# A state-space mixer on one core: decay exponents formed by accumulating DMA transfers instead of matmuls, their exponentials moved to other places in ScalarE's order, all convolved tiles gated through Tanh

## The chip, the cores and the metric

One NeuronCore of one Trainium2 chip. The kernel is one launch. The metric is the device time of that launch in microseconds (us), as the median over runs; a profiled execution has its own time and its own span (first to last instruction).

## What is computed

Two transformer-like blocks run one after the other on 256 tokens of width 1024, all in float32: six feed-forward parts on the main stream, one on a context stream, an attention and recurrence mixer, a gated convolution mixer and a state-space mixer (SSD) with a Fourier branch. The change lies in the state-space mixer alone. Its core, per direction, cut to what matters:

```
xbc = silu(centred_conv3(xbc, conv_w) + conv_b)          # split in cm, xs, bm
dt  = softplus(dt_raw + dt_bias);  a = -exp(a_log)
a_cs = cumsum(dt * a)                                    # per head, inside chunks of 128 tokens
seg = exp(where(lower, a_cs[l] - a_cs[s], -inf))         # 128 x 128 per head, chunk, direction
cb  = einsum('lgn,sgn->gls', cm, bm)                     # 4 groups of 3 heads
y_diag = einsum('gls,grls,sgrp->lgrp', cb, seg, xs * dt)
y_off  = cm . h_prev . exp(a_cs)                         # what comes in from the other chunk and the context
y = y_f + flip(y_b) + d_skip * xs;  y = group_rms_norm(y * silu(z)) * w;  out = y @ w_out
```

12 heads of 64 columns in 4 groups, state size 128, 2 chunks of 128 tokens, 2 directions.

## The kernel before

All weights lie in one stream of 529 slots of 128 x 1024 float32 values (512 KB). SyncE loads a slot into one of 4 `raw` buffers. ScalarE rounds it to float32r (`w_hi<-raw`, L1145), VectorE takes the rest (`w_lo<-raw,w_hi`, L1784), into rings of 8 slots, and TensorE multiplies three times for each product (hi by hi, lo by hi, hi by lo). Each engine has one queue in program order; the order of every engine is written out by hand in one function for each of the eleven phases, and semaphores join them. `after_slots(n, k)` on ScalarE and VectorE prepares slots n+8 to n+7+k, once slots n to n+k-1 are used.

The phase `ssd` has 31 slots: 8 of `opening` (columns u and z), one for dt, 6 `x_slot` and 8 `state_slot` that give the transposed x, C and B columns in units 0 to 10 (units 0 to 2 have two tiles of 128 x 256, units 3 to 10 one tile), and 8 of the output projection (`down_slot`, L548). `x_slot` and `state_slot` are the TensorE line L518. The convolution of unit u is `centre(1, u)` on ScalarE (middle tap, from PSUM, L1535 and L1537) and `tapped(1, u)` on VectorE (two outer taps, L2270). Units 0 to 4 get their silu as half a tile times one plus its Tanh: `tanh(u)` on ScalarE (L1614), then `gated_tiles(u)` on VectorE (L2339). Units 5 to 10 get ACT.Silu on ScalarE (`silu_tile`, L1620).

The decays: `log_decays` leaves on TensorE the cumulated logs, by token (`logs`) and by head (rows of PSUM `tp`), which are split into a rounded part and the rest (`row_split_hi`, `rows_lower`, L1792). For each of 6 pairs of heads, `differences(r)` spreads a head's row over 128 partitions with a selecting matmul (L1012) and adds -1e30 outside the triangle with a second (L1013), for two heads, in one of two PSUM areas in turn; `decay(r)` on ScalarE is 8 exponentials of 128 x 128 (L1605) out of PSUM into `decays`. `both_ways(g)` (L2346) adds the two directions, `weighted(g)` (L2355) multiplies with `correlations(g)` (C times B, L1031). `far(g)` (L1049 to L1052) is the part from outside the chunk, `outputs(g)` (L1063) the part within. `far_scaled(g)` (L2368) adds the far part to `y_acc` in 12 instructions of 64 columns; `y_added(g)` (L2378, L2380) adds the near part and gates; then `squares(g)`, a root on GpSimd, `normed(g)` (L1644), `y_turned(b)` (L1075), `y_upper(b)`, `y_lower(b)` make the input of the output projection. GpSimd computes `later_states` (L2522), then the inputs `x_far` of `far` (L2528) and the skip term (L2531) in `far_inputs`.

## Time and profile before

| what | value |
|---|---|
| median of 3 runs | 1665.7 us (1664.59 to 1666.12) |
| profiled execution | 1665.99 us, span 1664.2 us |
| granted TensorE clock | 0.999 of full speed in the mean |
| TensorE, VectorE, ScalarE, GpSimd busy | 99%, 74%, 56%, 9% of the span |
| phase `ssd` in the trace | from about 1355 us to 1473 us |

Each group of rows further down is one view of that one execution. Times are from the span's start. A row of an engine in order of time can join several instructions (x8): then its length goes from the first one's start to the last one's end. Instructions of one engine overlap a little, so that a row's length is more than its share of the queue.

### The profile page before, as it was taken

To read this page: it belongs to the slowest core of one execution; us is meant where nothing else is said; L and a number is where in the kernel's file an instruction comes from. 1 tells how busy PE (TensorE), PEld (TensorE's weight loads), DVE (VectorE), ACT (ScalarE), POOL (GpSimd) and SP (SyncE) were. 2 spreads that over 40 slices of the span, in tenths; PEclk is the share of its full clock that TensorE was granted. 3 is DMA by queue.
4 is the path that set the end of the run, shared out by engine and by line. 5 is a ranking of instruction groups with operands and counts; after the bars stand their busy time and mean duration, and the time that the engine had idled before them with its cause. 6 is when DMAs were issued, how large, how long until landed. Compare 5 with 4: busy or idle time off the path is not lost.

```text
span 1664.2 us, 22774 instructions
## 1 busy us (share of the span) xinstructions
PE 1655.0 (99%) x8740; PEld 1414.7 (85%) x8740; DVE 1228.9 (74%) x1632; ACT 926.2 (56%) x1396; POOL 153.3 (9%) x210
## 2 busy tenths in 40 slices
PE   9999999999999999999999999999999999999998
PEld 7888888888888888888899888888888889988887
DVE  6888776788888777776688876655766668986564
ACT  6655577645555455555566455554645458664553
POOL 1100100000211001020010011000002011311000
PEclk9999999999999999999999999999999999999999
DMA  8977553788859876687545557654667546357551
GB/s 300 329 268 259 166 193 102 254 287 258 284 174 332 261 251 216 248 305 259 193 167 187 168 172 265 202 187 141 230 209 253 185 134 203 110 182 239 190 189 64
DMA packets 99356, 358.47 MB, mean 215 GB/s; under 512 B 11184, under 2 KB 11696, under 8 KB 99248
## 3 DMA queue, kind: packets, MB, share of 16 engines
q1 hardware_dynamic: 92736, 334.73, 59.5%
q0 software_dynamic: 6368, 22.21, 4.4%
q8 instruction: 69, 1.13, 0.3%
q14 instruction: 39, 0.32, 0.1%
q10 hardware_dynamic: 144, 0.07, 0.0%
HBM read 355.85 MB, written 1.12 MB: 215 GB/s over the span
## 4 chain that ended last, share of the span: by engine, by line
PE 94%; DVE 3%; DMA 2%; ACT 1%; issue 1%; SPq 0%; DVEq 0%; POOLq 0%; POOL 0%; ACTq 0%
PE dn L548 28%; PE gu L503 19%; PE gu L537 10%; PE tp L537 10%; PE gu L536 5%; PE tp L536 5%; PE dn L518 4%; PE gu L533 1%; PE tp L533 1%; DMA raw<-in_weights 1%; PE tp L466 1%; PE dn L537 1%; PE gu L534 1%; PE tp L534 1%; PE dn L503 1%
## 5 line engine op out<-in xcount | busy, mean ns | idle before, releaser
L1784 DVE TENSOR_TENSOR w_lo<-raw,w_hi 128x1024 fp32r<-128x1024 f32 x518 | 637.3, 1241 | 216.1 <-ACT w_hi L1145 211.2
L1145 ACT ACTIVATE w_hi<-raw 128x1024 fp32r<-128x1024 f32 x520 | 547.9, 1057 | 323.9 <-PE dn L548 148.5
L503 PE MATMUL gu<-w_hi,hT 128*128 128x512 f32 x1056 | 329.0, 393 | 1.2 <-DVE w_lo L1777 0.8
L537 PE MATMUL gu<-hT,w_hi 128*128 128x512 f32 x728 | 259.5, 396 | 0.0
L537 PE MATMUL tp<-hT,w_hi 128*128 128x512 f32 x728 | 259.5, 396 | 0.0
L548 PE MATMUL dn<-w_hi,actT_hi 128*128 128x512 f32 x608 | 238.8, 393 | 0.0
L548 PE MATMUL dn<-w_lo,actT_hi 128*128 128x512 f32 x608 | 236.9, 390 | 0.0
L548 PE MATMUL dn<-w_hi,actT_lo 128*128 128x512 f32 x608 | 236.8, 389 | 0.0
L503 PEld LDWEIGHTS gu<-w_hi,hT 128*128 128x128 f32 x1056 | 195.5, 188 | 42.8 <-DVE w_lo L1784 1.6
L503 PE MATMUL gu<-w_lo,hT 128*128 128x512 f32 x528 | 205.8, 390 | 0.0
L536 PE MATMUL gu<-hT,w_lo 128*128 128x256 f32 x728 | 203.1, 279 | 0.0
L536 PE MATMUL tp<-hT,w_lo 128*128 128x256 f32 x728 | 203.0, 279 | 0.0
L537 PEld LDWEIGHTS gu<-hT,w_hi 128*128 128x128 f32 x728 | 136.6, 188 | 28.2
L537 PEld LDWEIGHTS tp<-hT,w_hi 128*128 128x128 f32 x728 | 136.6, 188 | 28.2
L536 PEld LDWEIGHTS tp<-hT,w_lo 128*128 128x128 f32 x728 | 137.2, 189 | 4.7
L536 PEld LDWEIGHTS gu<-hT,w_lo 128*128 128x128 f32 x728 | 137.2, 189 | 4.5
L548 PEld LDWEIGHTS dn<-w_lo,actT_hi 128*128 128x128 f32 x608 | 114.2, 188 | 24.2
L548 PEld LDWEIGHTS dn<-w_hi,actT_lo 128*128 128x128 f32 x608 | 114.2, 188 | 23.5
L1928 DVE CUSTOM_DVE_ANT_0 arena<-arena 128x1024 f32<-128x1024 f32 x112 | 133.3, 1217 | 0.3
L548 PEld LDWEIGHTS dn<-w_hi,actT_hi 128*128 128x128 f32 x608 | 114.1, 188 | 21.2
L503 PEld LDWEIGHTS gu<-w_lo,hT 128*128 128x128 f32 x528 | 99.1, 188 | 21.0
L2484 POOL TENSOR_SCALAR ms<-ssq 128x1 f32<-128x1 f32 x42 | 20.5, 488 | 929.4 <-ACT junk L1179 915.9
(366 smaller groups left out, 2091.5 us busy)
## 6 DMA issues: line engine op xcount, KB each, us to landing
raw<-in_weights SPq DMA_DIRECT2D x561, 512.0 KB, 4.3
arena<-in_ada_w SPq DMA_DIRECT2D x72, 512.0 KB, 4.4
post_row<-in_post_rows POOLq DMA_DIRECT2D x10, 512.0 KB, 5.8
pre_row<-in_pre_rows POOLq DMA_DIRECT2D x10, 512.0 KB, 6.8
mod_row<-mod POOLq DMA_DIRECT2D x9, 512.0 KB, 9.2
shift_row<-mod POOLq DMA_DIRECT2D x5, 512.0 KB, 9.3
x<-in_x_in SPq DMA_DIRECT2D x4, 256.0 KB, 5.8
arena<-in_c_rows POOLq DMA_DIRECT2D x2, 512.0 KB, 8.9
```

What stands on the lines that cost most here:

```text
L466: m = pe.transpose(in_bank(s, t, half)[:, q * P:(q + 1) * P], rows[:, t, k * P:(k + 1) * P], ident[:])
L503: m = pe.matmul(bank, h[:, k, t * P:(t + 1) * P], w[:, r, kk * 512:(kk + 1) * 512], start=k == 0 and q == 0, stop=k == KT - 1 and q == 2)
L518: m = pe.matmul(o, w[:, r, k * P:(k + 1) * P], h[:, k, :], start=k == 0 and q == 0, stop=k == KT - 1 and q == 2)
L533: pe.matmul(o, w_hi[:, r, c], hT[:, :, k, :], start=True, stop=False)
L534: pe.matmul(o[:, 0:TOK], w_lo[:, r, c], hT_hi[:, k, :], start=False, stop=False)
L536: pe.matmul(o[:, 0:TOK], w_lo[:, r, c], hT_hi[:, k, :], start=False, stop=False)
L537: m = pe.matmul(o, w_hi[:, r, c], hT[:, :, k, :], start=False, stop=k == KT - 1)
L548: m = pe.matmul(dn[:, t, c], a[:, k, :], w[:, r, c], start=start and q == 0, stop=stop and q == 2)
L1145: act.activation(o, i, ACT.Copy, **kw).then_inc(done, 1)
L1784: dve.tensor_tensor(w_lo[:, r, :], raw[:, n % RAW, :], w_hi[:, r, :].bitcast(F32), ALU.subtract).then_inc(lo_ready, 1)
L1928: m = dve.tensor_tensor_reduce(ada_out[:, v, :], w, c_row[:, v, :], 1.0, 0.0, ALU.mult, ALU.add, mod_cols[:, i, v:v + 1])
L2484: pool.tensor_scalar(ms[:, c], ssq[:, c, 0], eps, None, ALU.add).then_inc(pool_step, 1)
```

## The change

- The rows of cumulated logs (12 x 512) are copied to SBUF and stored in DRAM (`row_store`) by a DMA that ScalarE issues. Six GpSimd DMAs (`rows_spread`) read two rows each, spread them over 128 partitions and add them in place onto `decays`, where a mask (0 or -1e30) was loaded during `ffn_4` by six more GpSimd DMAs. `decay(r)` now reads SBUF and waits for its transfer. `differences`, the split of the rows and the tiles made for it are gone.
- `decay(0)` to `decay(5)` stand later in ScalarE's order, one after each of several slots, up to behind `normed(1)`.
- All eleven units go through Tanh and `gated_tiles`; `silu_tile` is gone.
- `far_inputs` and the skip term (`skipped`) move from GpSimd to VectorE. `far_scaled(g)` is 4 wide instructions: two products out of PSUM into the used half of `decays`, two sums.
- TensorE takes `state_slot(8)` ahead of `outputs(0)`, and `state_slot(9)` ahead of `far(1)`.

```diff
-                def differences(r):
-                    if r == 0:
-                        pe.wait_ge(row_split, 1)
+                def x_tokens(t):
+                    if t:
+                        pe.wait_ge(four_ready, 3)
+                    else:
                         pe.wait_ge(p_ready, 2)
-                    elif r == 1:
-                        pe.wait_ge(four_ready, 3)
-                    elif r < 4:
-                        pe.wait_ge(dec_ready, 2 * (r - 1))
-                    else:
-                        pe.wait_ge(x_taken, r - 3)
-                    for q in range(2):
-                        h, bank = 2 * r + q, rows_bank(r)[:, q, :]
-                        pe.matmul(bank, select[:, h:h + 1].broadcast_to([P, P]), log_rows, start=True, stop=False)
-                        m = pe.matmul(bank.rearrange("p (d t c) -> p d t c", d=2, t=TT), unit,
-                                      outside.unsqueeze(2).broadcast_to([P, 2, TT, P]), start=False, stop=True)
-                    m.then_inc(rows_psum, 1)
-
-                def x_tokens(t):
-                    pe.wait_ge(dec_ready, 2 * (3 + t))
+                        pe.wait_ge(rows_taken, 1)
                     for i in range(SSD_W // P):
                         m = turned_tile(tok_bank(t)[:, i * P:(i + 1) * P], 1, XS_T + i, t)
                     m.then_inc(tokT_psum, 1)
...
                 def correlations(g):
+                    pe.wait_ge(xbc_ready, XBC_BEFORE[1] + X_UNITS + 2 * (g + 1))
                     if g:
-                        pe.wait_ge(state_tiles, 2 * g)
                         pe.wait_ge(g_ready, g)
                     else:
-                        pe.wait_ge(xbc_ready, XBC_BEFORE[1] + TANH_UNITS)
-                        pe.wait_ge(dec_ready, 10)
+                        pe.wait_ge(x_taken, 1)
...
@@ -1086,30 +1074,24 @@
                 log_decays(1)
                 fourier_mixed()
                 x_slot(1, 1)
-                differences(0)
                 x_slot(2, 0)
-                differences(1)
                 x_slot(2, 1)
-                differences(2)
                 state_slot(3)
-                differences(3)
                 state_slot(4)
                 pe.wait_ge(xbc_ready, XBC_BEFORE[1] + X_UNITS)
                 x_tokens(0)
                 x_tokens(1)
                 state_slot(5)
-                differences(4)
                 state_slot(6)
-                differences(5)
                 correlations(0)
                 state_slot(7)
                 far(0)
+                state_slot(8)
                 outputs(0)
                 correlations(1)
-                state_slot(8)
+                state_slot(9)
                 far(1)
                 outputs(1)
-                state_slot(9)
                 correlations(2)
                 state_slot(10)
                 far(2)
...
                 def decay(r):
-                    act.wait_ge(rows_psum, r + 1)
+                    act.wait_ge(rows_added[r], 16)
                     for q in range(2):
                         h = 2 * r + q
                         for t in range(TT):
                             for d in range(2):
                                 at = slice(d * TOK + t * P, d * TOK + (t + 1) * P)
-                                m = act.activation(decays[:, h, at], rows_bank(r)[:, q, at], ACT.Exp,
+                                m = act.activation(decays[:, h, at], decays[:, h, at], ACT.Exp,
                                                    bias=shifts[:, t * NDT + d * SSD_H + h:t * NDT + d * SSD_H + h + 1])
...
-                copy(log_rows, tp[:, 1, :], row_split_hi)
+                copy(log_rows, tp[0:SSD_H, 1, :], rows_taken)
+                act.wait_ge(rows_taken, 1)
+                act.dma_start(row_store, log_rows).then_inc(rows_stored, 16)
                 act.wait_ge(four_psum, 3)
                 copy(f_out, gu[:, 1, :].rearrange("p (f c) -> p f c", f=2), four_ready)
                 tanh(0)
                 centre(1, 1, x0 + 3)
                 after_slots(x0 + 3, 1)
-                act.wait_ge(shift_ready, 1)
-                decay(0)
...
                 act.activation(exps[:, 0:2 * NDT], logs[:, 0:2 * NDT], ACT.Exp).then_inc(p_exp, 1)
                 after_slots(x0 + 4, 1)
-                decay(1)
                 tanh(1)
                 centre(1, 2, x0 + 5)
                 after_slots(x0 + 5, 1)
-                decay(2)
                 tanh(2)
-                decay(3)
                 centre(1, 3, s0)
                 after_slots(s0, 1)
+                act.wait_ge(shift_ready, 1)
+                decay(0)
                 centre(1, 4, s0 + 1)
...
-                decay(4)
+                decay(1)
                 centre(1, 6, s0 + 3)
+                cb_taken(0)
                 after_slots(s0 + 3, 1)
-                decay(5)
-                cb_taken(0)
-                copy(actT_hi[:, :, :], f_out, mix_hi)
-                silu_tile(5)
-                silu_tile(6)
+                decay(2)
                 centre(1, 7, s0 + 4)
                 after_slots(s0 + 4, 1)
-                cb_taken(1)
+                tanh(5)
+                tanh(6)
+                copy(actT_hi[:, :, :], f_out, mix_hi)
                 centre(1, 8, s0 + 5)
                 after_slots(s0 + 5, 1)
+                cb_taken(1)
+                decay(3)
                 squares(0)
-                silu_tile(7)
-                silu_tile(8)
+                centre(1, 9, s0 + 6)
                 normed(0)
-                centre(1, 9, s0 + 6)
+                tanh(7)
+                tanh(8)
+                after_slots(s0 + 6, 1)
+                decay(4)
                 cb_taken(2)
-                after_slots(s0 + 6, 1)
                 squares(1)
-                silu_tile(9)
                 centre(1, 10, s0 + 7)
+                after_slots(s0 + 7, 1)
+                tanh(9)
+                tanh(10)
                 normed(1)
-                silu_tile(10)
-                after_slots(s0 + 7, 1)
+                decay(5)
                 cb_taken(3)
                 squares(2)
...
+                def far_inputs():
+                    dve.wait_ge(x_taken, TT)
+                    dve.wait_ge(state1_ready, 1)
+                    for d in range(2):
+                        w = far_rate[:, d * SSD_H:(d + 1) * SSD_H].unsqueeze(2).broadcast_to([P, SSD_H, SSD_P])
+                        dve.tensor_tensor(by_head(x_far[d]), by_head(x_tok[:, d, :]), w, ALU.mult).then_inc(far_ready, 1)
+
+                def skipped():
+                    for t in range(TT):
+                        w = ssd_rows[:, 2 * NDT:].unsqueeze(2).broadcast_to([P, SSD_H, SSD_P])
+                        dve.tensor_tensor(by_head(y_acc[:, t, :]), by_head(x_tok[:, t, :]), w, ALU.mult).then_inc(skip_ready, 1)
+
                 def far_scaled(g):
+
+                    heads = slice(g * HPG, (g + 1) * HPG)
                     dve.wait_ge(yoff_psum, g + 1)
                     if g == 0:
                         dve.wait_ge(p_exp, 4)
-                        dve.wait_ge(skip_ready, 2)
+                    for t in range(TT):
+                        w = exps[:, t * NDT:(t + 1) * NDT].rearrange("p (d h) -> p d h", d=2)[:, :, heads]
+                        dve.tensor_tensor(far_parts(g)[:, t, :, :, :], gu[:, t, 0:2 * GW].rearrange("p (d j c) -> p d j c", d=2, j=HPG),
+                                          w.unsqueeze(3).broadcast_to([P, 2, HPG, SSD_P]), ALU.mult).then_inc(yoff_used, 1)
+                    dve.wait_ge(yoff_used, TT * (g + 1))
+                    dve.wait_ge(skip_ready, 2)
+                    acc = y_acc[:, :, g * GW:(g + 1) * GW].rearrange("p t (j c) -> p t j c", j=HPG)
                     for d in range(2):
-                        for t in range(TT):
-                            for j in range(HPG):
-                                w = t * NDT + d * SSD_H + g * HPG + j
-                                acc = y_acc[:, t, g * GW + j * SSD_P:g * GW + (j + 1) * SSD_P]
-                                c = d * GW + j * SSD_P
-                                m = dve.scalar_tensor_tensor(acc, gu[:, t, c:c + SSD_P], exps[:, w:w + 1], acc, ALU.mult, ALU.add)
-                            if d:
-                                m.then_inc(yoff_used, 1)
+                        m = dve.tensor_tensor(acc, far_parts(g)[:, :, d, :, :], acc, ALU.add)
                         if d == 0:
                             then(m)
+                    m.then_inc(far_added, 1)
...
@@ -2408,38 +2387,46 @@
                 after_slots(x0 + 3, 2)
                 gated_tiles(1)
                 tapped(1, 2)
-                both_ways(0)
                 after_slots(x0 + 5, 1)
                 gated_tiles(2)
-                both_ways(1)
                 tapped(1, 3)
                 after_slots(s0, 1)
                 tapped(1, 4)
                 after_slots(s0 + 1, 1)
                 gated_tiles(3)
                 gated_tiles(4)
+                far_inputs()
                 tapped(1, 5)
                 after_slots(s0 + 2, 1)
-                both_ways(2)
+                both_ways(0)
                 tapped(1, 6)
                 weighted(0)
                 after_slots(s0 + 3, 1)
-                dve.wait_ge(mix_hi, MIX0["ssd"] + 1)
-                lower(actT_lo[:, :, :], f_out, actT_hi[:, :, :], mix_lo)
                 tapped(1, 7)
+                gated_tiles(5)
+                gated_tiles(6)
+                skipped()
                 far_scaled(0)
+                both_ways(1)
                 y_added(0)
                 weighted(1)
                 after_slots(s0 + 4, 1)
                 tapped(1, 8)
+                dve.wait_ge(mix_hi, MIX0["ssd"] + 1)
+                lower(actT_lo[:, :, :], f_out, actT_hi[:, :, :], mix_lo)
                 after_slots(s0 + 5, 1)
+                tapped(1, 9)
+                gated_tiles(7)
+                gated_tiles(8)
                 far_scaled(1)
-                both_ways(3)
                 y_added(1)
-                tapped(1, 9)
+                both_ways(2)
                 weighted(2)
                 tapped(1, 10)
+                gated_tiles(9)
+                gated_tiles(10)
                 far_scaled(2)
+                both_ways(3)
                 y_added(2)
                 weighted(3)
                 far_scaled(3)
...
+            def rows_spread():
+                pool.wait_ge(rows_stored, 16)
+                for r in range(PAIRS):
+                    pool.wait_ge(outside_in[r], 16)
+                    pool.dma_start(decays[:, 2 * r:2 * r + 2, :], row_store[2 * r:2 * r + 2, :].partition_broadcast(P),
+                                   accum_op=ALU.add).then_inc(rows_added[r], 16)
...
+                    for r in range(PAIRS):
+                        pool.wait_ge(slot_used, BASE[name] + 32 + 3 * r)
+                        pool.dma_start(decays[:, 2 * r:2 * r + 2, :], small["outside"].unsqueeze(1).broadcast_to([P, 2, 2 * TOK])).then_inc(outside_in[r], 16)
...
+        "outside": np.stack([np.where(i[:, None] <= i[None, :], 0.0, -1e30)] * TT + [np.where(i[:, None] >= i[None, :], 0.0, -1e30)] * TT, axis=1).reshape(P, 2 * TOK),
```

TensorE between two column slots, where `differences(3)` stood; before:

```order
L518 MATMUL dn<-hT,w_lo 128x256
L1012 MATMUL gu<-actT_hi,actT_lo 128x512 [waits dec_ready]
L1013 MATMUL gu<-actT_lo 128x512
L1012 MATMUL gu<-actT_hi,actT_lo 128x512
L1013 MATMUL gu<-actT_lo 128x512
L518 MATMUL dn<-hT,w_hi 128x256 [waits lo_ready,conv_done]
```

The same place now (the line L518 has become L520):

```order
L520 MATMUL dn<-hT,w_lo 128x256
L520 MATMUL dn<-hT,w_hi 128x256 [waits lo_ready,conv_done]
```

Four matmuls of 512 columns and a wait for ScalarE are gone between the slots, here and at five other places.

VectorE from the outer taps of unit 8 on, before (L2270 taps, L2368 far part, L2346 both directions, L2378 and L2380 `y_added(1)`):

```order
L2270 SCALAR_TENSOR_TENSOR arena<-dn,ssd_cols,arena 128x255 [waits xbc_evac]
L2270 SCALAR_TENSOR_TENSOR arena<-dn,ssd_cols,arena 128x255 [waits dve_step]
L1784 TENSOR_TENSOR w_lo<-raw,w_hi 128x1024 [waits hi_ready]
L2368 SCALAR_TENSOR_TENSOR arena<-gu,dt_tmp,arena 128x64 [waits yoff_psum]
L2368 SCALAR_TENSOR_TENSOR arena<-gu,dt_tmp,arena 128x64 x5
L2368 SCALAR_TENSOR_TENSOR arena<-gu,dt_tmp,arena 128x64 [waits dve_step]
L2368 SCALAR_TENSOR_TENSOR arena<-gu,dt_tmp,arena 128x64 x5
L2346 TENSOR_TENSOR arena<-arena 128x3x256 [waits dec_ready]
L2378 TENSOR_TENSOR arena<-tp,arena 128x2x192 [waits y_psum,yoff_used]
L2380 TENSOR_TENSOR arena<-arena,xn 128x2x192 [waits y_taken]
```

And now (L2246 taps, L1763 `w_lo`, L1771 the low part of the Fourier output, L2305 `gated_tiles` of units 7 and 8, L2343 and L2349 the far part):

```order
L2246 SCALAR_TENSOR_TENSOR arena<-dn,arena 128x255 [waits xbc_evac]
L2246 SCALAR_TENSOR_TENSOR arena<-dn,arena 128x255 [waits dve_step]
L1771 TENSOR_TENSOR actT_lo<-junk,actT_hi 128x512 [waits mix_hi]
L1763 TENSOR_TENSOR w_lo<-raw,w_hi 128x1024 [waits hi_ready]
L2246 SCALAR_TENSOR_TENSOR arena<-dn,arena 128x255 [waits xbc_evac]
L2246 SCALAR_TENSOR_TENSOR arena<-dn,arena 128x255 [waits dve_step]
L2305 SCALAR_TENSOR_TENSOR arena<-act_tok,arena 128x256 [waits tanh_ready] x2
L2343 TENSOR_TENSOR arena<-gu,dt_tmp 128x2x3x64 [waits yoff_psum]
L2343 TENSOR_TENSOR arena<-gu,dt_tmp 128x2x3x64
L2349 TENSOR_TENSOR arena<-arena 128x2x192 [waits skip_ready,yoff_used]
L2349 TENSOR_TENSOR arena<-arena 128x2x192 [waits dve_step]
```

The taps of unit 9 and the gating of units 7 and 8 now stand ahead of the far part of group 1, and the far part is 4 instructions where it was 12.

ScalarE from the middle tap of unit 8 on, before (L1620 silu of units 7 and 8, L1644 `normed(0)`):

```order
L1537 ACTIVATE arena<-dn,ssd_cols 128x256 [waits slot_used]
L1145 ACTIVATE w_hi<-raw 128x1024 [waits slot_used,landed_3]
L1636 ACTIVATE arena,gstat<-arena 128x192 [waits y_gated]
L1636 ACTIVATE arena,gstat<-arena 128x192
L1620 ACTIVATE arena<-arena,ssd_cols 128x256 [waits conv_done] x2
L1644 ACTIVATE arena<-arena,gstat 128x192 [waits gr_ready]
```

And now (L1587 `decay(3)`, L1613 `squares(0)`, L1517 middle tap of unit 9, L1621 `normed(0)`, L1596 `tanh(7)` and `tanh(8)`):

```order
L1127 ACTIVATE silu<-tp 128x256 [waits cb_psum]
L1587 ACTIVATE arena<-arena,dt_tmp 128x128 [waits rows_added_3]
L1587 ACTIVATE arena<-arena,dt_tmp 128x128 x7
L1613 ACTIVATE arena,gstat<-arena 128x192 [waits y_gated]
L1613 ACTIVATE arena,gstat<-arena 128x192
L1517 ACTIVATE arena<-dn,arena 128x256 [waits slot_used]
L1621 ACTIVATE arena<-arena,gstat 128x192 [waits gr_ready]
L1621 ACTIVATE arena<-arena,gstat 128x192
L1596 ACTIVATE act_tok<-arena 128x256 [waits xbc_ready,conv_done] x2
```

The exponentials of a pair stand ahead of the squares, and the activations of units 7 and 8 behind `normed(0)`, where they stood ahead of it.

## Rows read from the trace of the kernel before

**Rows 1.** The page: TensorE's busy time, share of the span, instructions.

```profile
PE 1655.0 (99%) x8740; PEld 1414.7 (85%) x8740; DVE 1228.9 (74%) x1632; ACT 926.2 (56%) x1396; POOL 153.3 (9%) x210
```

**Rows 2.** Waits of TensorE in the whole span: total us, times, longest.

```profile
PE dn L603 <- DVE actT_hi L2458: 1.5, 1, 1.5
```

**Rows 3.** A stretch of the mixer: busy us (instructions) of each engine, then granted clock.

```profile
1440.00:1450.00 10.00, 10.00 (x70) 9.65 (x70) 8.67 (x27) 5.96 (x18) 2.12 (x5) 1.00 0.00 0
```

**Rows 4.** Chain that ended last: start us, length us, what.

```profile
1396.78 0.37 PE tp L1012
...
1420.79 0.23 PE gu L1013
...
1421.89 2.86 PE dn L518 x24
```

**Rows 5.** VectorE in order of time: start us, length us, instruction, [idle before].

```profile
1388.59 2.33 DVE L2258 TENSOR_TENSOR arena<-dt,neg_a 128x48 f32<-128x48 f32 x1
...
1391.84 2.35 DVE L1784 TENSOR_TENSOR w_lo<-raw,w_hi 128x1024 fp32r<-128x1024 f32 x2
...
1395.92 0.68 DVE L1792 TENSOR_TENSOR actT_hi<-tp,actT_hi 12x512 fp32r<-12x512 f32 x1
...
1401.61 4.90 DVE L1784 TENSOR_TENSOR w_lo<-raw,w_hi 128x1024 fp32r<-128x1024 f32 x2
...
1410.79 0.75 DVE L2339 SCALAR_TENSOR_TENSOR arena<-act_tok,arena 128x256 f32<-128x256 f32 x2
1411.46 0.95 DVE L2346 TENSOR_TENSOR arena<-arena 128x768 f32<-128x768 f32 x1
...
1416.42 3.31 DVE L2339 SCALAR_TENSOR_TENSOR arena<-act_tok,arena 128x256 f32<-128x256 f32 x2
...
1420.56 1.59 DVE L1784 TENSOR_TENSOR w_lo<-raw,w_hi 128x1024 fp32r<-128x1024 f32 x1
1422.07 2.22 DVE L2346 TENSOR_TENSOR arena<-arena 128x768 f32<-128x768 f32 x1
...
1431.18 0.56 DVE L2378 TENSOR_TENSOR arena<-tp,arena 128x384 f32<-128x384 f32 x1
...
1449.19 2.52 DVE L2368 SCALAR_TENSOR_TENSOR arena<-gu,dt_tmp,arena 128x64 f32<-128x64 f32 x12 [0.96 <-PE gu L1049]
...
1480.29 0.41 DVE L1983 TENSOR_TENSOR act_tok<-silu,gu 128x256 f32<-128x256 f32 x1
```

**Rows 6.** GpSimd in order of time, same columns.

```profile
1379.17 0.92 POOL L2537 DMA_DIRECT2D mod_row<-mod  x1
1388.46 2.39 POOL L2539 TENSOR_TENSOR post_row<-post_row,mod_row 128x1024 f32<-128x1024 f32 x1 [8.37 <-DMA mod_row<-mod]
...
1402.97 2.46 POOL L2522 TENSOR_TENSOR shift_row<-state,dt_tmp 128x768 f32<-128x768 f32 x1
1415.98 3.47 POOL L2528 TENSOR_TENSOR arena<-arena,dt_tmp 128x768 f32<-128x768 f32 x2 [10.55 <-ACT arena L1145]
```

**Rows 7.** ScalarE in order of time, same columns.

```profile
1394.57 1.28 ACT L1614 ACT_TABLE_LOAD   x1
1395.92 0.72 ACT L1614 ACTIVATE act_tok<-arena 128x256 f32<-128x256 f32 x2
...
1401.99 2.23 ACT L1605 ACTIVATE arena<-gu,dt_tmp 128x128 f32<-128x128 f32 x8
...
1455.70 0.81 ACT L1644 ACTIVATE arena<-arena,gstat 128x192 f32<-128x192 f32 x2 [1.14 <-POOL gstat L2593]
...
1478.67 0.38 ACT L1294 ACTIVATE silu<-gu 128x256 f32<-128x256 f32 x1 [0.34 <-PE gu L503]
```

**Rows 8.** DMA issues: target, source, queue, count, KB each, median us to landing.

```profile
arena<-in_ada_w SPq DMA_DIRECT2D x72, 512.0 KB, 4.4
...
mod_row<-mod POOLq DMA_DIRECT2D x9, 512.0 KB, 9.2
...
mod<-dt_tmp POOLq DMA_DIRECT2D x3, 24.0 KB, 3.4
```

70 lines of the change are left out of this document (23 added, 47 removed).

## Prediction

> **What bounds the kernel now.** The page comes first: TensorE is busy for 99% of the span [rows 1]. The waits of TensorE say whether that busy time has holes: the longest of all is 1.5 us, at the kernel's start [rows 2]. The chain of waits through the mixer runs from matmul to matmul [rows 4]. So the kernel lasts as long as its matmuls, and work on other engines is hidden, until it isn't. How much room they have is read from a stretch late in the mixer: between 1440 and 1450 us TensorE has no idle time, and VectorE is busy for 8.67 of the 10 us [rows 3]. The trace of VectorE in order of time shows how near it is: the far part of group 3 at 1449.19 us is the first place for long at which it waits for TensorE, and it waits 0.96 us [rows 5]. It was ready at 1448.23. **The room that VectorE leaves to TensorE in this phase is about 1 us.** That number decides this case.
>
> **What the change takes from TensorE.** `differences` is 24 matmuls of 512 columns. In the chain of waits they are 24 pieces, of which the first and the last are shown, 0.37 and 0.23 us [rows 4]: 0.37 + 23 x 0.23 = 5.7 us, all on the path. Nothing is added there; the four matmuls that give the rows keep their 128 columns. If all else stays hidden the profiled 1666.0 us become 1660.3.
>
> **What it does to VectorE**, counted from 1382 us to the moment at which it is ready for the far part of group 3:
> - Preparing tiles and the second product of dt with the rates go. That product took 2.33 us for 48 columns, since GpSimd's product of 1024 columns ran from 1388.46 for 2.39 us [rows 5, 6]. Without them the short work is done before GpSimd starts, and the `w_lo` that begins at 1391.84 can begin at 1388.46 + 2.39 = 1390.85 at the earliest: -1.0.
> - The split of the rows: -0.7 (0.68, at 1395.92) [rows 5].
> - `far_inputs` leaves GpSimd, where it held VectorE up from 1415.98 on [rows 6]. Two gated tiles took 3.31 instead of 0.75, one `w_lo` 1.59 where two take 2.35 at 1391.84, `both_ways` 2.22 instead of 0.95 [rows 5]: 2.56 + 0.4 + 1.27 = -4.2.
> - The far part, three times: 2.52 us now. The new form is not in the trace. Nearest is the sum out of PSUM over 384 columns, 0.56 [rows 5]: four of these less overlap, with three waits for an own result, about 2.15. -0.35 each, -1.0. Bounds: no saving, and -1.8 if each costs 0.48.
> - Added: `x_far` and the skip term, four products of 768 columns. Nearest: `both_ways`, 0.95, or 0.87 of the queue. +3.5.
> - Added: units 5 to 10 are gated here, six tiles at half of 0.75 less overlap, 0.34 [rows 5]: +2.0.
> - `later_states` stays on GpSimd. It stretches two `w_lo` from 2.35 to 4.90 [rows 5, 6]. Now six DMA issues stand ahead of it, at 0.92 each by the row of `mod_row` [rows 6], 5.5 us from about 1398 on, so it starts some 2 us later than before. It costs 2.55 again; below, nothing, if it falls beside other work.
>
> Sum: -6.9 + 5.5 = -1.4. TensorE is 5.7 us shorter, VectorE's queue 1.4 us.
>
> **What it does to ScalarE.** The six `decay` stay at 2.23 us or less each (8 exponentials) [rows 7]; out of SBUF they may be a little shorter, I take no gain. What counts is who stands behind them. `decay(0)` now stands ahead of the middle tap of unit 4, `squares(0)` (which needs VectorE) ahead of that of unit 9, `normed(0)` ahead of the Tanh of 7 and 8. VectorE needs these taps and Tanhs in turn, so it gains waits inside its queue. I take 0.8 us for them; below, 0, above, one whole decay, 2.2. The later places for the decays themselves are no gain.
>
> The Silu table that `silu_tile` loaded now has to be loaded at the next feed-forward part, ahead of the activation at 1478.67 us. A load takes 1.28 us [rows 7], the idle 0.34 before that activation absorbs some of it, the activation ends near 1480.0, and VectorE takes its tile at 1480.29 [rows 5]: hidden, 0. The Trainium skill (ScalarE: Activation LUTs, What ACT_TABLE_LOAD costs) counts a drain of about 1380 ns more for each switch, 2.66 us in all; this would be an estimate of +1.1 us behind VectorE's turn. The trace does not show that drain, since the Tanh after the load at 1394.57 starts 1.35 us later, at 1395.92 [rows 7], and I keep 0.
>
> **The transfers.** Six masks during `ffn_4` and six additions in the mixer, 512 KB each. In the first, weights have room: 72 transfers of the same size for `ada_w` ran beside the weights [rows 8] and TensorE never waited [rows 2]. 0. In the mixer, ScalarE has copied the rows when it loads a table at 1394.57 [rows 7]; a small store takes 3.4, the issue of the first addition 0.92, and a plain transfer of the same kind lands in 9.2 at the slowest [rows 6, 8]: 1408.1. `decay(0)` stands behind the Tanh of unit 2, whose tile VectorE gates at 1410.79 now [rows 5] and would gate 2 to 2.5 us earlier, so it is reached near 1409. 0, with 1 us in hand. An accumulating transfer is not in the trace.
>
> **The sum.** VectorE would be ready for the far part of group 3 at 1448.23 - 1.4 + 0.8 = 1447.6, and TensorE, if never held, would have delivered it at 1443.5. So TensorE is held, and this point, 1449.19 before, moves by 1.6 us. The rest of the phase is a chain through all engines: far part, gating, squares, root, `normed(3)`, which ended 1455.70 + 0.81 = 1456.5 [rows 7], just ahead of the transposes that need it. It moves with it. 1665.99 - 1.6 = 1664.4; the median of the runs lies 0.3 below the profiled execution: **1664.1 us**. TensorE gives 4.1 of its 5.7 us back in new waits. The largest I expect at `correlations(2)`: it needs units 7 and 8 gated, and on VectorE those stand behind `w_lo`, the taps of unit 9 and, through ScalarE, behind `squares(0)` and `normed(0)`; 2 us or more.
>
> A difference below 0.2% (3.3 us) can't be told from none here. The likeliest case by itself: with `later_states` harmless (-2.6) 1661.5; with no saving in the far part (+1.0) and waits of 2.2 (+1.4) 1666.5.
>
> **Rivals.**
> - *Everything hidden.* VectorE's lateness has slack that its queue order doesn't show, since much of what it does is prepared ahead. For: 8 slots of weights lie ready. Against: 0.96 us is all that it waited. 1665.7 - 5.7 = 1660.0. Chance 0.18.
> - *The additions land late (slower).* An accumulating transfer must read its target too. If it takes twice 9.2 us it lands at 1417.3, 8.3 after `decay(0)` is reached, and ScalarE, which is in order, holds the middle tap of unit 4 and its `w_hi` for that long: 1664.1 + 8.3 = 1672.4. It decides from a landing of 10.1 us on; the kernel is slower by 3.3 us from one of 15.0 on. Chance 0.11.
> - *The clock falls in the new waits (slower).* The granted clock stands at 1.00, that is 2.4 GHz [rows 3], and no idle of TensorE was over 1.5 us [rows 2]. After one of 3 to 4 us it might stand at 1.2 GHz for a time; each column slot of 24 matmuls, 2.86 us [rows 4], would take as much again. Two such slots give 1664.1 + 5.7 = 1669.8. The Trainium skill (TensorE: Matmul & The Clock Gate, Why this matters for your kernels) warns of idle gaps between bursts of matmuls for this reason; no run here shows it. Chance 0.06.
> - *No difference by another way*, the table's drain among them (1665.2): 0.05.
>
> The forecast keeps 0.60. The first rival and the forecast's lower end (0.06) make **faster 0.24**; the late transfers (0.11), the fallen clock (0.05, the rest of it costs too little) and what adds up above the forecast (0.02) make **slower 0.18**; **same 0.58**. The range 1660.0 to 1669.5 leaves out the late transfers and the far end of the clock.
>
> **What would show it.** Right: no L1012 and L1013; TensorE waits for VectorE in the mixer, 3 to 5 us together, the most at the third pair of correlations; gated tiles and `both_ways` at 0.75 and 0.95 in all places but beside `later_states`; VectorE without a wait of 1 us before the last far part; clock 1.00. Wrong: a mixer shorter by over 4 us (VectorE's queue has slack); waits of ScalarE for a transfer; products of 768 columns well off 0.95; far parts at 2.5 or more.

## The result and the profile after

The changed kernel takes 1668.1 us in the median of 20 runs (1665.84 to 1670.45), the kernel before 1665.61 us in 20 runs on the same chip. The ratio is 1.0014, 95% interval 1.0008 to 1.0020: 0.14% slower, 2.5 us between the medians. That is more than the runs' own uncertainty and less than the 0.2% set as the bound, so by the bound it is no change, and on the other side of it than forecast. The forecast was 1664.1 us. The profiled execution of the changed kernel took 1669.41 us, its span is 1667.6 us.

The waits of TensorE in the mixer, where [rows 2] had none (engine, line, what it waited for, then us in total, times, longest; L1019 is `correlations`, L1051 `outputs`; such a wait is called a stop below):

```profile
PE tp L1019 <- DVE arena L2305: 3.8, 1, 3.8
PE tp L1051 <- DVE arena L2321: 0.8, 2, 0.4
```

L2305 is `gated_tiles`. The stop of 3.8 us is at `correlations(2)`, which waits for units 7 and 8 to be gated. Around it, the busy time by stretches (columns as in [rows 3]: length, busy time of PE, PEld, DVE, ACT and POOL, granted clock, DMA share, GB/s):

```profile
1430.00:1434.00 4.00, 3.35 (x24) 2.92 (x22) 3.93 (x7) 1.48 (x6) 1.78 (x2) 1.00 0.00 0
1434.00:1436.00 2.00, 0.00 (x0) 0.00 (x0) 2.00 (x4) 1.85 (x5) 0.12 (x1) 1.00 0.74 262
1436.00:1438.00 2.00, 0.50 (x1) 0.50 (x2) 1.96 (x6) 2.00 (x7) 0.00 (x0) 0.58 0.55 160
1438.00:1440.00 2.00, 2.00 (x7) 1.64 (x7) 1.90 (x4) 1.23 (x4) 0.00 (x0) 0.50 0.25 102
1440.00:1442.00 2.00, 2.00 (x12) 2.00 (x11) 1.86 (x4) 0.80 (x4) 0.25 (x2) 0.50 0.00 0
1442.00:1444.00 2.00, 2.00 (x14) 2.00 (x14) 0.68 (x1) 0.00 (x0) 0.70 (x1) 0.72 0.00 0
1444.00:1446.00 2.00, 2.00 (x15) 2.00 (x14) 1.02 (x3) 1.90 (x4) 0.00 (x0) 1.00 0.04 8
```

TensorE stands still from 1433.7 to 1437.5 us; before the end of that the granted clock falls from 1.00 to 0.50, the level of 1.2 GHz, and it is back at 1.00 by 1444. The chain of waits shows what that costs, and a second thing:

```profile
1436.69 0.76 DVE arena L2305 x2
1437.46 0.04 issue
1437.50 2.08 PE tp L1019 x4
1439.58 4.50 PE dn L520 x24
...
1444.57 1.05 ACT w_hi L1127
1445.62 0.18 ACT act_tok L1596
1445.80 0.03 issue
1445.82 0.40 ACT act_tok L1596
1446.22 0.69 ACT arena L1621 x2
1446.91 2.35 ACT arena L1587 x8
...
1451.22 0.96 DVE arena L2321
1452.18 0.04 issue
1452.23 1.55 PE tp L1051 x12
```

The same chain in the kernel before, at the third pair of correlations (L1031) and at `outputs(3)` (L1063):

```profile
1437.94 0.86 PE tp L1031 x4
...
1449.15 1.28 PE tp L1063 x12
```

The four matmuls of `correlations(2)` take 2.08 us now and the 24 of `state_slot(10)` 4.50, together 6.58. In the kernel before, at full clock, the four took 0.86 and a slot 2.86 [rows 4]: 2.9 us lost. And since `state_slot(10)` ends late, so do, on ScalarE, the middle tap of unit 10, a weight slot, the Tanhs, `normed(1)` and `decay(5)` behind them (L1587), and VectorE's `both_ways(3)` and `weighted(3)` behind that. `outputs(3)` starts at 1452.23, 3.1 us later than in the kernel before.

VectorE in the same phase (start, length, engine, line, tiles; in brackets the idle time before). These rows answer to [rows 5]:

```profile
1388.15 0.21 DVE L2236 TENSOR_TENSOR dta<-dt,neg_a 128x48 f32<-128x48 f32 x1
1389.40 0.43 DVE L2296 TENSOR_TENSOR silu<-gu,junk 128x258 f32<-128x258 f32 x1 [0.82 <-ACT junk L1127]
1390.07 3.64 DVE L1763 TENSOR_TENSOR w_lo<-raw,w_hi 128x1024 fp32r<-128x1024 f32 x2
1400.16 2.42 DVE L1763 TENSOR_TENSOR w_lo<-raw,w_hi 128x1024 fp32r<-128x1024 f32 x2
1404.14 1.78 DVE L2246 SCALAR_TENSOR_TENSOR arena<-dn,arena 128x255 f32<-128x255 f32 x4 [0.89 <-ACT arena L1517]
1405.84 1.83 DVE L1763 TENSOR_TENSOR w_lo<-raw,w_hi 128x1024 fp32r<-128x1024 f32 x1
1410.91 1.00 DVE L2246 SCALAR_TENSOR_TENSOR arena<-dn,arena 128x255 f32<-128x255 f32 x2 [0.53 <-ACT arena L1517]
1412.84 1.22 DVE L1763 TENSOR_TENSOR w_lo<-raw,w_hi 128x1024 fp32r<-128x1024 f32 x1 [0.93 <-ACT w_hi L1127]
1414.55 0.76 DVE L2305 SCALAR_TENSOR_TENSOR arena<-act_tok,arena 128x256 f32<-128x256 f32 x2 [0.48 <-ACT act_tok L1596]
1415.22 1.82 DVE L2328 TENSOR_TENSOR arena<-arena,dt_tmp 128x768 f32<-128x768 f32 x2
1423.42 1.00 DVE L2246 SCALAR_TENSOR_TENSOR arena<-dn,arena 128x255 f32<-128x255 f32 x2 [0.55 <-ACT arena L1517]
1424.67 0.76 DVE L2305 SCALAR_TENSOR_TENSOR arena<-act_tok,arena 128x256 f32<-128x256 f32 x2 [0.25 <-ACT act_tok L1596]
1425.35 1.82 DVE L2333 TENSOR_TENSOR arena<-arena,ssd_rows 128x768 f32<-128x768 f32 x2
...
1444.70 1.00 DVE L2246 SCALAR_TENSOR_TENSOR arena<-dn,arena 128x255 f32<-128x255 f32 x2 [2.02 <-ACT arena L1517]
```

Up to 1424.7 VectorE waits seven times for ScalarE, 4.45 us together (0.82, 0.89, 0.53, 0.93, 0.48, 0.55, 0.25). From there to the gated unit 8, at 1437.44, it works 12.8 us without a pause, so the stop of TensorE ends with that queue. The longest wait of all, 2.02 us before 1444.70, comes behind the stop and is a part of the second chain above. The work itself got less: from 1386 us to `outputs(3)` VectorE is busy 57.6 of 66 us here and 60.9 of 63 before. It did 3.3 us less and still came late.

One more hint lies in the runs. Of the 20, 14 had a mean granted clock of 0.997 and took 1668.64 us in the mean; 5 had 0.999 and took 1666.48; the one at 0.998 took 1667.0.

### The profile page after: what moved, and what is told of

It reads as the page before. It is cut to its first block, busy times and chain, and to the rows that moved or that the text cites. A ratio compares the mean times of both kernels' runs of the same rounds, so it can differ in the third digit from the quotient of the medians.

```text
span 1667.6 us, 22716 instructions
## 1 busy us (share of the span) xinstructions
PE 1653.5 (99%) x8716; PEld 1412.3 (85%) x8716; DVE 1225.7 (74%) x1604; ACT 927.9 (56%) x1396; POOL 154.6 (9%) x218
## 3 DMA queue, kind: packets, MB, share of 16 engines
q8 instruction: 69, 1.13, 0.3%
## 4 chain that ended last, share of the span: by engine, by line
PE 90%; DVE 4%; DMA 3%; ACT 2%; issue 1%; SPq 0%; DVEq 0%; POOLq 0%; POOL 0%; ACTq 0%
PE dn L550 28%; PE gu L505 19%; PE gu L539 10%; PE tp L539 10%; PE gu L538 5%; PE tp L538 5%; DMA raw<-in_weights 3%; PE dn L520 2%; PE gu L535 1%; PE tp L535 1%; DVE w_lo L1763 1%; PE tp L468 1%; PE dn L539 1%; PE gu L536 1%; PE tp L536 1%
## 5 line engine op out<-in xcount | busy, mean ns | idle before, releaser
L1763 DVE TENSOR_TENSOR w_lo<-raw,w_hi 128x1024 fp32r<-128x1024 f32 x518 | 636.0, 1238 | 217.9 <-ACT w_hi L1127 213.3
## 6 DMA issues: line engine op xcount, KB each, us to landing
arena<-row_store POOLq DMA_DIRECT2D x6, 512.0 KB, 16.6
```

The costliest lines, as they stand in the source:

```text
L1763: dve.tensor_tensor(w_lo[:, r, :], raw[:, n % RAW, :], w_hi[:, r, :].bitcast(F32), ALU.subtract).then_inc(lo_ready, 1)
```

## The experiments

Three theories. **Order and clock**: the queues of VectorE and ScalarE stop TensorE at `correlations(2)`, and the stop costs clock besides. **Transfers**: the accumulating transfers load the DMA engines (share 1.00 in 1397 to 1421 us against 0.51 before) and the weights come late. **TensorE's saving was worth less** than 5.7 us. All runs were timed against the kernel before on the same chip; the ratio is the measure, since the kernel before itself was at 1665.3 to 1665.9 us.

| kernel | median us | ratio to before | 95% interval |
|---|---|---|---|
| changed | 1668.1 | 1.0014 | 1.0008 to 1.0020 |
| e1_order | 1666.72 | 1.0005 | 0.9996 to 1.0013 |
| e2_fill | 1666.85 | 1.0004 | 0.9995 to 1.0013 |
| e3_plain | 1669.46 | 1.0019 | 1.0010 to 1.0028 |
| e4_pool | 1667.36 | 1.0007 | 0.9999 to 1.0016 |
| e5_both | 1666.56 | 1.0006 | 0.9997 to 1.0015 |
| e6_decay5 | 1666.11 | 1.0005 | 0.9997 to 1.0014 |
| e7_again (changed) | 1669.11 | 1.0018 | 1.0010 to 1.0027 |
| e8_refill | 1670.33 | 1.0031 | 1.0020 to 1.0043 |
| e9_fill2 | 1665.99 | 1.0000 | 0.9991 to 1.0009 |
| e10_silu | 1664.79 | 0.9995 | 0.9986 to 1.0003 |
| e11_silu10 | 1665.18 | 0.9997 | 0.9988 to 1.0006 |
| e12_nofill | 1666.89 | 1.0006 | 0.9997 to 1.0015 |

**1. The stop without the fall of the clock.** Matmuls without a use in the stop:

```diff
                 outputs(1)
+                pe.wait_ge(conv_done, XBC_BEFORE[1] + 7)
+                for k in range(8):
+                    pe.matmul(any_bank(2)[:, TOK:2 * TOK], xbc[:, BM_T + 1, 0:P], xbc[:, CM_T + 1, :], start=True, stop=True)
                 correlations(2)
```

> The changed kernel, with 8 matmuls of 128 x 256 in an unused half of a PSUM bank ahead of correlations(2) on TensorE (by the row of 0.86 us for 4 instructions some 3.4 us), so that TensorE works through most of the 3.8 us in which it waits there. Their result is not used. Nothing is sooner for it. Theory (the granted clock falls because TensorE stops): the clock stays at 1.00 in 1430 to 1450, correlations(2) takes 0.86 us and state_slot(10) 2.87 us instead of 2.08 and 4.50, and the kernel gets faster by 2 to 3 us, to 1665.5 to 1666.5, though it does more work. Rival (the stop alone costs, and the clock is no part of it, or falls for another reason): the rows at 1437 to 1444 stay at 2.08 and 4.50 us and the time stays at 1668 or rises.

The stretches of e2_fill at the same place:

```profile
1436.00:1438.00 2.00, 2.00 (x10) 1.52 (x8) 1.96 (x5) 2.00 (x6) 0.00 (x0) 1.00 0.47 154
1438.00:1440.00 2.00, 1.70 (x11) 1.47 (x11) 1.93 (x6) 2.00 (x8) 0.00 (x0) 1.00 0.63 244
1440.00:1442.00 2.00, 2.00 (x19) 2.00 (x18) 1.93 (x4) 0.34 (x3) 0.00 (x0) 1.00 0.03 8
```

and the filling and `correlations(2)` in its trace of TensorE:

```profile
1434.45 3.67 PE L1097 MATMUL dn<-arena 128*128 128x256 f32 x16
1438.42 1.13 PE L1019 MATMUL tp<-arena 128*128 128x256 f32 x4 [0.30 <-DVE arena L2308]
```

The clock stays at 1.00, and `state_slot(10)` ends at 1442.26 although `correlations(2)` starts 0.9 us later than in the changed kernel. From the start of `correlations(2)` to the end of the slot it takes 3.84 us here and by the same view 6.40 in the changed kernel (1437.50 to 1443.90), so 2.6 of the 2.9 us are the clock's; behind a stop the four matmuls take 1.13 for 0.86 us even at clock 1.00. With 3.4 us more work for TensorE the ratio is 1.0004 for 1.0014, a gain of 1.7 us (1.2 between the medians, which come from two chips), short of the 2 to 3 expected. The two intervals overlap a little, so this pair alone is not quite certain; the two under 6 point the same way. So the clock is a cost of its own, and not all of the loss: `outputs(3)` still starts at 1450.97, behind `decay(5)`.

**2. The stop itself.** Two pieces of order, on ScalarE and VectorE:

```diff
                 cb_taken(1)
+                tanh(7)
                 decay(3)
                 squares(0)
                 centre(1, 9, s0 + 6)
+                tanh(8)
                 normed(0)
-                tanh(7)
-                tanh(8)
...
                 weighted(1)
-                after_slots(s0 + 4, 1)
                 tapped(1, 8)
+                gated_tiles(7)
                 dve.wait_ge(mix_hi, MIX0["ssd"] + 1)
                 lower(actT_lo[:, :, :], f_out, actT_hi[:, :, :], mix_lo)
-                after_slots(s0 + 5, 1)
+                gated_tiles(8)
+                after_slots(s0 + 4, 2)
                 tapped(1, 9)
-                gated_tiles(7)
-                gated_tiles(8)
```

> The changed kernel with two pieces of order moved and nothing else: ScalarE takes tanh(7) ahead of decay(3) and tanh(8) ahead of normed(0); VectorE takes tapped(8), gated_tiles(7), the rest of the Fourier output and gated_tiles(8) ahead of the two slot preparations and tapped(9). Theory (the late gated tiles stop TensorE 3.8 us at correlations(2), and the stop lets the granted clock fall, which costs some 2.8 us more in the profiled run): the wait at correlations(2) falls from 3.8 to about 1 us, the granted clock stays at 1.00 in 1430 to 1450, the kernel takes 1664 to 1665.5 us, below the changed kernel's 1668.1 by 2.5 to 4. Rival (the accumulating transfers load the DMA engines and the weights come late): the wait goes to another place, the time stays within 1 us of 1668.1. Rival (the 24 matmuls were worth less than 5.7 us): the wait shrinks and the time stays above 1666.

The stop at `correlations(2)` shrinks to 0.63 us. But `outputs(2)` then waits 2.02 us for `weighted(2)`, the clock in 1440 to 1450 falls to 0.83, and the kernel is at 1666.7, above what the theory gave: VectorE's queue goes on without a pause to 1443. The stop was moved and cut, not removed. A wait that shrinks while the time stays above 1666 is also what the second rival said; section 5 takes it up.

**3. The transfers.** The six transfers overwrite the mask in place of adding to it:

```diff
-                copy(log_rows, tp[0:SSD_H, 1, :], rows_taken)
+                copy(log_rows, tp[0:SSD_H, 1, :], rows_taken, scale=0.0, bias=-1.0e4)
...
-                    pool.dma_start(decays[:, 2 * r:2 * r + 2, :], row_store[2 * r:2 * r + 2, :].partition_broadcast(P),
-                                   accum_op=ALU.add).then_inc(rows_added[r], 16)
+                    pool.dma_start(decays[:, 2 * r:2 * r + 2, :], row_store[2 * r:2 * r + 2, :].partition_broadcast(P)).then_inc(rows_added[r], 16)
```

> The changed kernel with the six transfers onto the decays as plain ones of the same shape that overwrite the mask, and rows of one constant, so that the exponentials get finite numbers; the decays are then not the reference's. Theory (the order of VectorE and ScalarE makes the stop): the transfers land sooner than 16.6 us and load the DMA engines less in 1397 to 1421, the stop at correlations(2) stays between 3.3 and 3.9 us, and the time stays within 1 us of 1668.1. Rival (the accumulation costs the loss, by late weights): the stop shrinks below 2.5 us and the kernel takes 1666 us or less.

DMA from 1395 to 1432 us (q0 is GpSimd's queue: packets, MB, share of 16 engines; then issues, size, median us to landing), of the changed kernel:

```profile
q0 software_dynamic: 864, 3.15, 46.0%
...
raw<-in_weights SPq DMA_DIRECT2D x9, 512.0 KB, 10.3
arena<-row_store POOLq DMA_DIRECT2D x6, 512.0 KB, 16.6
```

and of e3_plain:

```profile
q0 software_dynamic: 864, 3.15, 23.4%
...
raw<-in_weights SPq DMA_DIRECT2D x9, 512.0 KB, 6.1
arena<-row_store POOLq DMA_DIRECT2D x6, 512.0 KB, 13.0
```

The additions and the weights beside them do land later, 16.6 and 10.3 us for 13.0 and 6.1. Yet the stop stays at 3.8 us, the clock falls behind it and the time doesn't fall: the transfers don't make the stop. The time is even somewhat above its range of 1 us, and the trace of VectorE says by what:

```profile
1400.63 2.39 DVE L1763 TENSOR_TENSOR w_lo<-raw,w_hi 128x1024 fp32r<-128x1024 f32 x2
1402.94 3.31 DVE L2305 SCALAR_TENSOR_TENSOR arena<-act_tok,arena 128x256 f32<-128x256 f32 x2
```

GpSimd issued the plain transfers in 3.23 us in all instead of 5.42, so that `later_states` came 1.7 us sooner and met the gated tiles of unit 1 (3.31 for 0.75); TensorE then waited 1.4 us at `x_tokens`. That new wait hides what the plain transfers may have gained elsewhere. For the adding ones do cost something that the prediction had not priced, the weights beside them: in the kernel before these landed in 3.6 us, and ScalarE never waited for one between 1397 and 1432 us; in the changed kernel it waited for weights 0.88, 0.24 and 0.64 us there, in e3_plain not at all. What that is worth in time is not shown.

**4. Who should do the four products.** `far_inputs` and the skip term back on GpSimd, behind `later_states`, as before:

```diff
-                far_inputs()
...
-                skipped()
...
                     later_states()
+                    far_inputs()
```

> The changed kernel with the inputs of far and the skip term back on GpSimd behind later_states, as in the kernel before. The prediction's balance had VectorE lose 3.5 us by taking these four products and gain 4.2 us by not being blocked by GpSimd's. By it: VectorE's preparations near 1410 to 1425 get longer, and the time goes from 1668.1 to 1668.3 to 1669.5. Rival (VectorE had no net gain by taking them, as it is the engine that is full here): the stop at correlations(2) shrinks by 1 us or more and the kernel takes below 1667.

The ratio is 1.0007 for 1.0014: the sign of the expectation was wrong. VectorE was stretched again, to 3.11, 1.59 and 2.23 us, as in [rows 5], but in a part (1413 to 1421 us) in which it otherwise waited for ScalarE; in return the 1.7 us of the skip term were gone from the part without a pause behind 1424, and the stop at `correlations(2)` was 2.2 us, with the clock at 1.00 in this execution, the fastest of its runs. A stop of 1.1 us at `correlations(0)` was new. The intervals of the two kernels overlap; the gain of about 1 us is likely, not certain.

With the order of e1_order added, and then `decay(5)` and `tanh(9)` ahead of `squares(1)` and `centre(10)`:

> The order of e1_order and, with it, the inputs of far and the skip term on GpSimd as in e4_pool. e1_order took the stop at correlations(2) away and got two new ones (2.0 us at outputs(2), clock 0.83 in 1440 to 1450), since VectorE worked without a pause from 1424 to 1443 in it. Theory (VectorE's work between 1424 and 1452 is now the bound, and each stop of some 2 us or more costs clock besides): taking the skip term's 1.7 us out of that stretch shortens the waits of TensorE below 1.5 us in all, the clock stays at 1.00, and the kernel takes 1665.0 to 1666.0 us. Rival (what GpSimd's products add to VectorE's instructions near 1413 to 1421, some 4 us, comes back later in full): 1666.5 us or more, as e1_order.

> e5_both with, on ScalarE, tanh(9) and decay(5) ahead of squares(1) and centre(10) instead of behind them, where ScalarE waited 2.5 us for TensorE in the changed kernel. Theory (behind the stops a second chain runs over ScalarE: centre(10), weights, tanh, normed(1), decay(5), both_ways(3), weighted(3), outputs(3)): outputs(3) no longer waits for decay(5), and the kernel takes 0.3 to 1 us less than e5_both. Rival (VectorE's own queue sets outputs(3)): within 0.3 us of e5_both, or above it, as squares(1) and centre(10) are later.

Neither could be told from e1_order (1.0006 and 1.0005). Both have a stop at `correlations(0)`, near 1416 (1.8 and 1.5 us, where GpSimd's products stretch VectorE's), and one of 1.55 us at `outputs(2)` near 1441, behind which the clock falls to 0.50 for some 3 us. So the rival of e5_both had its point: part of what GpSimd's products cost seems to have come back. In e6_decay5 `outputs(3)` no longer hangs on `decay(5)`, but on the chain from that stop.

**5. Is TensorE's saving real?** Work without a use where the differences stood, two matmuls of 0.43 us at each of the six places:

```diff
                 x_slot(1, 1)
+                for k in range(2):
+                    pe.matmul(any_bank(3)[:, TOK:2 * TOK], ident[:], tri[:, 0, 0, :], start=True, stop=True)
                 x_slot(2, 0)
```

> The changed kernel with TensorE's saved work put back as work without a use: two matmuls of 128 x 256 in full float32 (0.86 us by the row of correlations) at each of the six places where the two heads' differences stood, some 5.2 us in all. Theory (TensorE is not the bound in this part any more; VectorE's queue is): the stop at correlations(2) shrinks from 3.8 us to less than 1 us, the clock stays at 1.00 in 1430 to 1450, and the kernel is no slower than the changed one, 1666.5 to 1668. Rival (TensorE's saving is real in the time and the loss has come from elsewhere): the kernel gets slower by 2 us or more, to 1670 or above.

> The changed kernel once more, on the chip of the other three, with a second profile of it. Theory (the clock falls in most of its executions, and costs what lies between them): 1667.5 to 1668.7 us in the median, and the executions with a mean granted clock of 0.999 are faster by 1.5 to 2 us than those with 0.997. Rival (the spread has nothing to do with the clock): no such difference.

Against the changed kernel on the same chip (1669.11), 5.2 us of work cost 1.2 us between the medians and 2.2 us by the ratios (1.0031 for 1.0018). So 3 to 4 of them fell into waits. TensorE's work was neither free, as the theory had it, nor was all of it in the time; the rival's 2 us and 1670 lie at the edge of what was measured. The stop at `correlations(2)` was 2.3 us and the clock was lost all the same (0.84 in 1440 to 1450). In the repeat of the changed kernel the clock did not part the runs as it had: 1668.93 us in 7 runs at 0.997, 1668.31 in 3 at 0.998, and a single one at 0.999 with 1669.12. In two other kernels it did: e3_plain took 1669.75 us in the mean of 6 runs at 0.997 and 1668.00 in 5 at 0.999, e12_nofill (below) 1667.39 in 8 at 0.998 and 1664.62 in 2 at 0.999.

**6. Holding the clock in the better order.** e9_fill2 is e6_decay5 with three matmuls of 0.43 us without a use ahead of `outputs(2)` and of `correlations(3)`. e10_silu takes units 9 and 10 back to ScalarE's Silu, so that VectorE no longer gates them, with `centre(10)` ahead of `decay(5)`, and fills ahead of `outputs(2)` alone (against e6_decay5):

```diff
-                tanh(9)
-                decay(5)
-                squares(1)
                 centre(1, 10, s0 + 7)
-                tanh(10)
+                decay(5)
+                silu_tile(9)
+                squares(1)
+                silu_tile(10)
...
                 far(2)
+                pe.wait_ge(conv_done, XBC_BEFORE[1] + 8)
+                for k in range(3):
+                    pe.matmul(any_bank(3)[:, TOK:2 * TOK], ident[:], tri[:, 0, 0, :], start=True, stop=True)
                 outputs(2)
```

> e6_decay5 with three matmuls of 128 x 256 without a use (0.43 us each, 1.3 us) ahead of outputs(2) and three ahead of correlations(3), the two places where TensorE still stops 1.5 us. In e6_decay5 what follows these stops ran at the low clock: outputs(2) 2.11 us for 1.28, correlations(3) 1.93 for 0.86, 6 matmuls of the output projection 1.54 for 1.37. Theory (short stops following on each other let the clock fall, and the clock is what keeps this order behind the kernel before): the clock stays at 1.00 in 1440 to 1450, the kernel gets 1 to 2 us faster than e6_decay5 (1666.1), to 1664 to 1665, below the kernel before. Rival (the spread and the median of e6_decay5 come from other places): within 0.5 us of it, or above it by the work added.

> e9_fill2 with units 9 and 10 back on ScalarE's Silu (as in the kernel before) in place of Tanh and VectorE's gating, centre(10) ahead of decay(5), and no filling ahead of correlations(3). VectorE has two instructions of 0.34 us less ahead of weighted(3), and correlations(3) waits for ScalarE alone; ScalarE has a table load (1.28 us in the trace of before) more in a stretch in which it was busy half of the time. Theory (VectorE's queue sets outputs(3)): 0.5 to 1 us less than e9_fill2. Rival (the table load and the silu come late, since squares(1) and normed(1) stand behind them): no gain, or 0.5 us more.

> e10_silu with silu(10) ahead of squares(1) on ScalarE. In e10_silu correlations(3) started at 1442.46 behind silu(10) (1442.01), which stood behind the 0.78 us of squares(1), while tapped(10) had ended at 1441.1. Theory (that chain is what is left of the stops): correlations(3) starts up to 0.7 us sooner, the kernel takes 0.3 to 0.7 us less than e10_silu on the same chip. Rival (VectorE's weighted(3), which ended at 1446.0 for a start of outputs(3) at 1446.94, or normed(1) behind it takes over): within 0.3 us.

> e10_silu without the three matmuls without a use ahead of outputs(2). Theory (they hold the clock through the stop there and cost nothing, as TensorE would wait): outputs(2) and correlations(3) run in part at the low clock again, the mean clock is 0.998, and the kernel takes 0.5 to 1.5 us more than e10_silu. Rival (with fewer stops around, the clock holds without them, or the filling itself is on the path): the same time or up to 1 us less.

e10_silu and e12_nofill differ in three matmuls. The chain of e12_nofill:

```profile
1444.32 2.07 PE tp L1019 x4
1446.39 1.92 PE dn L550 x6
```

and of e10_silu:

```profile
1439.50 0.02 issue
1439.52 1.28 ACT L1605
1440.80 0.01 issue
1440.81 0.39 ACT arena L1605
...
1442.46 1.13 PE tp L1019 x4
1443.59 1.39 PE dn L550 x6
```

Without them, waits of 1.5 us at `outputs(2)` and 0.6 at `correlations(3)` were followed by a clock of 0.50 in 1444 to 1446 us, and the same ten matmuls took 3.99 us instead of 2.52. The ratios are 1.0006 and 0.9995, so 1.3 us of useless work are worth about 1.8 us. Here too the intervals overlap, but all three pairs with and without filling differ in the same direction (e2_fill, e9_fill2 and e10_silu lie 0.0010, 0.0005 and 0.0011 below the kernels they fill). e10_silu is the fastest kernel here, clearly faster than the changed one; its interval against the kernel before takes in 1. It gained 0.8 us by the ratios over e9_fill2 on the same chip, as its theory had it. e9_fill2 gained less than the 1 to 2 us expected over e6_decay5, and its expectation had misread the trace: the second stop of e6_decay5 was at `correlations(0)`, not ahead of `correlations(3)`, so the filling there lay on the path. Its clock held in 1440 to 1450; in the profiled execution, its slowest, it fell behind a stop of 2.3 us at `correlations(0)` instead. e11_silu10, with `silu_tile(10)` ahead of `squares(1)`, gained nothing: `correlations(3)` was sooner, but then `far(3)` waited 0.7 us for ScalarE behind `normed(1)`, the case its rival named.

## Why the prediction was wrong

The forecast was 1.6 us faster, and the kernel became 2.5 us slower. That 1668.1 still lies in the range of 1660.0 to 1669.5 is due to the width of the range and not to the sum behind it.

*TensorE's work, -5.7 us*: as said. L1012 and L1013 are gone. *The room, about 1 us*: right, 0.96 in [rows 5].

*How much comes back in waits, 4.1 us, most of it at* `correlations(2)`: right in place and nearly in size, 3.8 + 0.8 = 4.6 us. e8_refill says the same from the other side: 3 to 4 of 5.2.

**The step that failed first: "The clock falls in the new waits", kept at 0.06 and out of the sum.** The sum itself had a stop of 2 us and more at one place. It was priced by its length alone. The stop of 3.8 us took 2.6 us of clock with it in the profiled execution, in the pair of correlations and most of one slot, where the rival had two whole slots and 5.7 us; over the runs it is an estimated 1.2 to 1.7 us by e2_fill, 1.8 by e12_nofill against e10_silu, and 2.2 by the parting of the first 20 runs. The Trainium skill (TensorE: Matmul & The Clock Gate, Why this matters for your kernels) says that idle gaps between bursts of matmuls bring the throttle back; the trace agrees, 0.50 behind the stop. A rule that speaks against the very state one forecasts belongs in the sum.

**The second: "I take 0.8 us" for new waits in VectorE's queue, with 2.2 as the upper bound.** They were 4.45 us up to 1424.7, and 2.02 more behind the stop. VectorE began the far part of group 3 at 1452.09 us, forecast was 1447.6. The counting of the balance was at fault: gains early in the queue (-1.0 and -0.7 near 1390, -4.2 near 1416) were added up as if they reached its end. VectorE got ahead, and then waited for ScalarE, which waited for TensorE's slots, or had a decay or a late weight slot ahead of what VectorE needed. What decides is the work behind the last such wait, 12.8 us from 1424.7 to unit 8, and there the change added: the skip term 1.7 us, four of the gated tiles 1.4 and `both_ways(1)` 0.9, which had been done at 1411.46 before [rows 5], against 0.35 saved. A `w_lo` and the taps of unit 9, 2.0 us together, stood ahead of these gated tiles besides; e1_order, which puts them behind, cut the stop to 0.63 us. The forecast was off by 4.0 us in the median; the clock is an estimated 1.2 to 2.2 of them, and most of the rest belongs to this step.

The terms by themselves:
- The split of the rows, -0.7: gone. Together with the next term, -1.7 in all, it put the `w_lo` behind it at 1395.53 instead of 1396.85: -1.3.
- The rates and the preparations, -1.0: the product took 0.21 us, but GpSimd's long product then met the `w_lo` behind it (3.64 us for two) and VectorE had waited 0.82. Its taps of unit 0 began at 1393.63 instead of 1394.11: -0.5.
- `far_inputs` off GpSimd, -4.2: seen in the lengths (0.76, 1.22, 0.95), no gain in the time, by e4_pool likely a loss together with the products that VectorE took over.
- Products of 768 columns +3.5, gated tiles +2.0, far part -0.35 each: 1.82 for two, 0.76 for two, 1427.09 to 1429.21 for the first. Right.
- `later_states`, 2.55 kept: 0.7 (two `w_lo` at 2.42 for 2.35 us, one at 1.83 for 1.22), near the lower bound of nothing. The Trainium skill (SBUF — State Buffer, Who interferes with whom) says that VectorE and GpSimd lock a pair of ports that they share, and that the order of issue decides which of them is blocked. The trace agrees: here GpSimd's product of 24 columns, at 1401.27 us, met a `w_lo` of VectorE's that had begun before it and took 2.33 us, where it took 0.24 before.
- `decay` at 2.23 or less: 2.43 to 2.44 us out of SBUF. The guess that SBUF is no slower was wrong by 1.2 us over six. The Trainium skill (Perfetto Trace Analysis, Optimizing Scalar/DVE Operations) gives ScalarE about 93 ns of fixed cost on SBUF and 51 on PSUM; the trace has 26 ns more for each exponential out of SBUF, the same sign.
- The first addition: `decay(0)` ran at 1407.99 without waiting for it, forecast near 1409. Right, and the rival of late additions did not come.
- Masks in `ffn_4`, 0: in e4_pool, which has them, the product for dt in the mixer started at 1377.96 us, before at 1377.93. Right. The table, 0: nothing waited for it. In e10_silu, too, the Silu starts 1.29 us after its load does, without a drain.

The sum by what was measured, to the start of `outputs(3)`: -5.7 + 4.6 + 2.9 + 0.3 (the phase began later in this execution) leaves about 1.0 of the 3.1 us. Of this some 0.3 are matmuls behind a wait, `outputs(1)` taking 1.55 for 1.28 us; the rest was not followed up. Before the clock is counted the change is thus worth about nothing, not -1.6. The five runs at 0.999 (1666.48) say nothing or a little loss, against 1665.61.

What stays open: which stops cost the clock. It held in e4_pool behind one of 2.19 us at `correlations(2)` and behind stops at `correlations(0)` of 1.77 in e5_both and 1.49 in e12_nofill. It fell in e8_refill behind one of 2.27 and in e5_both and e6_decay5 behind one of 1.55 at `outputs(2)`. What the late weights cost, and the last part of the sum above, are open too. Whether e10_silu is faster than the kernel before is not settled either.

## What to carry to other kernels

When the bound engine loses work, ask at once where it will stop, and price each stop twice: its length, and the clock behind it. If the stop can't be removed, filling it with matmuls without a use can be the cheaper way. A balance of a queue is to be summed from its last wait for another engine on, not from its beginning: what is saved ahead of such a wait is gone. And work moved off a shared resource is only a gain if the place it goes to has room at that moment; here, by e4_pool, GpSimd's contention likely fell into time in which VectorE was idle anyway.
